# Order of the vector and scalar engines' work on the first two pairs of the up projection

## What is computed

```python
h = rms_norm_2(x, norm_mlp[l])
x = x + jnp.square(jax.nn.relu(h @ w_up[l])) @ w_down[l]
```

## Time and profile before

| | |
|---|---|
| median of 3 executions | 2404.96 us (2403.06 to 2407.01) |
| the profiled execution | 2402.84 us |
| its span, first to last instruction | 2401.0 us |
| TensorE busy in the span | 2358.2 us (98%) |
| VectorE, ScalarE, GpSimd busy | 1635.9, 1065.7, 963.7 us |
| granted TensorE clock, mean | 0.998 |

### The profile page before, as it was taken

How to read it: one execution, slowest core, us unless ns; L and a number is a source line. 1 busy time by engine, 2 the same in 40 slices (tenths; PEclk the granted TensorE clock), 3 DMA queues, 4 the chain that set the end, 5 groups by cost and what they waited for, 6 DMA issues and landing times.

```text
span 2401.0 us, 31551 instructions
## 1 busy us (share of the span) xinstructions
PE 2358.2 (98%) x11548; PEld 1871.2 (78%) x11548; DVE 1635.9 (68%) x2026; ACT 1065.7 (44%) x1628; POOL 963.7 (40%) x535
## 2 busy tenths in 40 slices
PE   9999999999999999999999999999999999999997
PEld 6888658887777777777788777788877888888886
DVE  6999975467647466475866555555688777637994
ACT  5555562335544545456442333223354444443344
POOL 2899833332222222222233111222346555465564
PEclk9999999999999999999999999999999999999999
DMA  3111333221111111111032111221125666886764
GB/s 138 44 44 52 105 140 123 79 95 45 45 41 41 41 41 45 41 41 41 27 113 66 49 40 35 82 71 45 53 114 155 153 153 160 227 294 238 276 240 146
DMA packets 112116, 238.76 MB, mean 99 GB/s; under 512 B 42360, under 2 KB 45304, under 8 KB 111992
## 3 DMA queue, kind: packets, MB, share of 16 engines
q1 hardware_dynamic: 73040, 216.28, 28.0%
q10 hardware_dynamic: 38952, 20.76, 3.9%
HBM read 184.44 MB, written 46.27 MB: 96 GB/s over the span
## 4 chain that ended last, share of the span: by engine, by line
PE 80%; DVE 8%; issue 4%; ACT 3%; POOL 3%; DMA 1%; ACTq 0%; SPq 0%; DVEq 0%; POOLq 0%
PE ps_A L897 23%; PE ps_B L897 22%; PE ps_A L1435 8%; PE ps_B L1435 8%; PE ps_C L1435 4%; PE ps_D L1435 2%; POOL ta L800 1%; PE ps_C L917 1%; PE ps_B L1179 1%; PE ps_D L1005 1%; PE ps_C L1071 1%; POOL accp L800 1%; PE ps_D L1071 1%; PE ps_D L1164 1%; PE ps_D L1152 1%
## 5 line engine op out<-in xcount | busy, mean ns | idle before, releaser
L774 POOL CAST w_hi<-w_raw 128x1024 fp32r<-128x1024 f32 x98 | 107.7, 1099 | 1059.1 <-PE ps_A L897 483.9
L767 POOL TENSOR_TENSOR w_lo<-w_raw,w_hi 128x1024 fp32r<-128x1024 f32 x124 | 307.4, 2479 | 49.6 <-ACT w_hi L1580 41.8
L862 POOL TENSOR_TENSOR down_w_lo<-d_raw,down_w_hi 128x512 fp32r<-128x512 f32 x112 | 179.3, 1620 | 136.1 <-ACT down_w_hi L2271 136.1
L897 PE MATMUL ps_A<-HA_hi,w_hi 128*128 128x512 f32 x640 | 201.2, 395 | 4.0 <-POOL w_lo L767 2.2
L897 PE MATMUL ps_B<-HA_hi,w_hi 128*128 128x512 f32 x640 | 202.2, 397 | 2.9 <-POOL w_lo L767 1.5
L897 PE MATMUL ps_B<-HA_lo,w_hi 128*128 128x512 f32 x640 | 197.5, 390 | 0.0
L897 PE MATMUL ps_A<-HA_lo,w_hi 128*128 128x512 f32 x640 | 197.4, 390 | 0.0
L897 PE MATMUL ps_B<-HA_hi,w_lo 128*128 128x512 f32 x640 | 197.3, 389 | 0.0
L897 PE MATMUL ps_A<-HA_hi,w_lo 128*128 128x512 f32 x640 | 197.3, 389 | 0.0
L897 PEld LDWEIGHTS ps_A<-HA_hi,w_hi 128*128 128x128 f32 x640 | 117.1, 188 | 29.7 <-issue 3.9
L897 PEld LDWEIGHTS ps_B<-HA_lo,w_hi 128*128 128x128 f32 x640 | 120.1, 188 | 25.6
(11 more groups left out here) (510 smaller groups left out, 5956.9 us busy)
## 6 DMA issues: line engine op xcount, KB each, us to landing
w_raw<-w_dram SPq DMA_DIRECT2D x124, 512.0 KB, 3.3
d_raw<-w_dram SPq DMA_DIRECT2D x64, 512.0 KB, 4.6
t_raw<-u_dram SPq DMA_DIRECT2D x56, 512.0 KB, 6.0
a_raw<-w_dram SPq DMA_DIRECT2D x32, 512.0 KB, 7.6
u_dram<-b SPq DMA_DIRECT2D x56, 256.0 KB, 5.2
u_dram<-t SPq DMA_DIRECT2D x48, 256.0 KB, 6.8
X<-x_dram SPq DMA_DIRECT2D x16, 512.0 KB, 7.1
d_raw<-w_dram SPq DMA_DIRECT2D x32, 256.0 KB, 3.0
```

Source lines behind the costliest of these rows:

```text
L767: pool.tensor_tensor(w_lo[q][:, :, :], w_raw[q][:, :, :], w_hi[q][:, :, :].bitcast(F32), ALU.subtract).then_inc(S[f"w_ready{q}"], 1)
L774: pool.tensor_copy(w_hi[q][:, :, :], w_raw[q][:, :, :]).then_inc(S["w_rounded"], 1)
L862: pool.tensor_tensor(lo[:, :, :], d_raw[i % 3][:, down_parts(x), :], hi[:, :, :].bitcast(F32), ALU.subtract).then_inc(S["down_split"], 1)
L897: op = pe.matmul(AB[b][:, cols], wt[:, w0 + k, :], act[:, k, cols], start=(first and k == ks[0] and step == 0), stop=(last and k == ks[-1] ...
```

## The change

On VectorE, `form_s2_s3(1)` moves from behind the last two activation splits to just behind `form_s4(0)`, ahead of the four `scaled_lo(3, j)`; it is given a wait for the sum (0,3), since it overwrites `s2`, which `form_s4(0)` reads. `form_t(0)` moves from the pass i = 1 of the loop (behind `c12_c21(0)`) into the pass i = 2, behind `c22(1)` and `r22(1)`. On ScalarE, `round_up(9)`, `(10)` and `(11)` each come one step sooner: 9 ahead of the first rounding of T2, 10 ahead of the second, and 11 ahead of the squares of pair 0 and `keep_p5(1)`. SyncE's, GpSimd's and TensorE's lists stay as they are.

```diff
             round_up(8)
+            round_up(9)
             round_two(4, T2[:, 0:2, :], 0)
-            round_up(9)
+            round_up(10)
             round_two(4, T2[:, 2:4, :], 1)
-            round_up(10)
             act.wait_ge(S["up_out"], OUT_AT[("c11", 0)] + 1)
             keep_p1(1)
+            round_up(11)
             squared(b11, 0, "r11")
             squared(b22, 0, "r22")
             keep_p5(1)
-            round_up(11)
...
             form_s4(0)
+            dve.wait_ge(S["up_sum"], SUM_AT[(0, 3)] + 1)
+            form_s2_s3(1)
             for j in range(KH):
                 scaled_lo(3, j, x_half(2 * j + 1, 1), 2 * j + 1)
...
-            form_s2_s3(1)
             next_cd()
...
                     r22(i - 1)
+                if i == 2:
+                    form_t(0)
                 form_s4(i)
                 c12_c21(i - 1)
-                form_t(i - 1)
+                if i > 1:
+                    form_t(i - 1)
                 if i < UP_PAIRS - 1:
                     form_s1(i + 1)
                     form_s2_s3(i + 1)
```

## The result

| | before | after |
|---|---|---|
| median (executions) | 2405.69 us (16) | 2410.24 us (16) |
| lowest to highest | 2402.43 to 2409.63 | 2408.92 to 2413.29 |
| span of the profiled execution | 2401.0 us | 2409.8 us |
| mean granted TensorE clock in it | 0.998 | 0.996 |

The ratio is 1.0020, 95% interval 1.0014 to 1.0027: slower by about 4.6 us, 0.19%. The two profiled spans are further apart, 8.8 us.

What follows compares the result with a forecast made beforehand. TensorE, with work in 98% of the span, was taken as the bound, hanging at product 18 on `form_t(0)`; 5.8 us of delay and 2.1 of clock made 7.9 us, median 2412.9 us, range 2406.5 to 2416.

Steps and rivals of the forecast that it cites:

- The chain: Up projection: product 18 hangs without slack on the end of `form_t(0)`, via stores, load of pair 3 and ScalarE; 15.06 us.
- Part 1: Head of the up projection: second pair's sums and roundings sooner; worth -0.25 us, bounds +0.4 and -1.6.
- Part 2: `form_t(0)` moved behind the read out of pair 1: ends at 1812.5, 5.8 us later; no stop before product 14.
- The count by turns: VectorE at `form_t(0)`: its four instructions take 2.7 us plus three turns with GpSimd's splits, after two turns ahead of it.
- The DMA term: Landing of the pair 3 loads behind the stores: change taken as 0, bounds -1 and +1 us.
- The clock: Behind the 8 us stop before product 18, TensorE falls to 1.2 GHz; return costs 2.1 us, bounds 0 and 3.
- The sum: Whole execution: 5.8 us of delay plus 2.1 of clock make 7.9 us, profiled 2410.7 us, median 2412.9.
- the milder rivals: Smaller losses: clock up or fewer turns, 2410 us, chance 0.25; VectorE ahead of GpSimd, 2405.8 us, chance 0.14.
- the forecast's own: Whole kernel: late `form_t(0)` and fallen clock as forecast, 2412.9 us, range 2410.5 to 2416, chance 0.55.
- rival 2: Same delay at product 18, but the clock stays up or VectorE meets fewer turns: 4 to 6 us, 2410 us, chance 0.25.
- The fourth: Faster: `form_t(0)` ends at 1807.5, load lands sooner, product 18 comes 0.3 to 0.8 us sooner; 2404.4 us, chance 0.06.
- the head's gain: Ahead of product 18, at the stops before products 10, 11 and 14: 1.7 us won, then swallowed by the stop.

Runs made afterwards that it cites:

- e1_after_loads_first: Changed kernel with SyncE issuing the two loads of pair 3 ahead of the five stores of pair 0; median 2405.09 us, ratio 1.0001 to the kernel before.
- e3_part2: Kernel before with only `form_t(0)` moved behind `c22(1)` and `r22(1)`; median 2410.51 us, ratio 1.0027 to the kernel before.
- e2_part1: Changed kernel with `form_t(0)` put back where it was; median 2404.51 us, ratio 0.9997 to the kernel before.
- e6_splits_behind: Changed kernel with ScalarE rounding operands 16 and 17 only behind the square of 12 of pair 1; median 2409.12 us, ratio 1.0016 to the kernel before.
- the filler: Changed kernel with 24 more matmuls, results unread, on TensorE right behind product 17; median 2408.68 us, ratio 1.0014 to the kernel before.
- e4_before_loads_first: Kernel before with SyncE issuing the loads of pair 3 ahead of the five stores of pair 0; median 2404.73 us, ratio 0.9997.

## Why the prediction was right, and where it was off

**The chain.** It was right in each link: product 18 hung on the end of `form_t(0)` through SyncE's queue and the load of pair 3, and `e1_after_loads_first` shows it by taking the load out, `e3_part2` by moving that step alone.

**Part 1** was put at -0.25 us, a small loss, and measured 0.0: in `e2_part1` product 11 starts at 36.72 instead of 36.79, and the median is level. The turning of a wait for GpSimd into one for VectorE came as told, product 9 stopping for both halves of its operand.

**Part 2, the end of `form_t(0)`.** Predicted 1812.5, 5.8 us late; measured 1813.43, less the 0.60 us by which the execution began later, 1812.83: 6.1 us late. The count by turns held, and `e6_splits_behind` shows that it is the turns. The Trainium skill, page "SBUF — State Buffer", section "Who interferes with whom", says that a VectorE instruction with two SBUF inputs and a GpSimd one that reads SBUF exclude each other for a whole instruction. The trace agrees: `form_t(0)` takes 5.8 us with three splits beside it and 3.7 with one. The split that took 4.09 us takes 4.08 us in the changed kernel too, and no run explains it.

**The DMA term** was mis-sized: I took 0 against the 9.7 us of the earlier trace rows, and the second load landed in 8.2 us, 1.5 us less (8.1 and 8.3 in `e3_part2` and `e6_splits_behind`, 9.7 in `e2_part1`, where `form_t(0)` stays). Why it lands sooner there is not shown. So the start of product 18 moved by 4.68 us, not 5.8.

**The clock** was put at 2.1 us, from the weight loads of the earlier trace rows. From product 18 to the start of the down projection the changed kernel took 2.77 us more than the kernel before, and with the filler nothing more. In `e3_part2` it took 2.07 us more, so the term varies. That the clock falls in all 16 executions is likely, since their mean clocks are 0.995 to 0.997, but the mean alone doesn't prove it: a quarter of the executions of the kernel before show 0.996 or 0.997 too. The Trainium skill, "TensorE: Matmul & The Clock Gate", section "HAM oscillation — how this bites in real kernels", says that waits between bursts of matmuls bring the clock down; here one wait of 6.55 us did.

**The sum** for one execution was 7.9 us; from the first product to the end it measured 8.20: 4.68 to product 18, 2.77 by the clock up to the beginning of the down projection, and 0.75 behind that, mostly in the stops there, which vary by as much from one execution of the kernel before to the next. That 7.9 and 8.20 are so close is in part luck: the DMA term was 1.5 us too high, the clock 0.7 too low, and the 0.75 was not in the sum. The step that failed is the last one: I carried the difference of single executions over to the medians, and the medians are only 4.6 us apart. The profiled execution of the kernel before lies 2.85 us under the median of its 16, that of the changed kernel 1.35 us above. The prediction took 2.12 us for the first, as for a fixed offset, and nothing for the second. A difference of two profiled executions carries the distance of both from their medians, here 4.2 us together. My range held the result only because it reached down to the milder rivals: 2410.24 us lies just under the forecast's own 2410.5 to 2416 and on the 2410 us of rival 2, though neither of that rival's conditions (a clock that stays up, fewer turns) came. The mechanism is the forecast's, the number is the rival's. Whether the change is slower by over 0.2%, to which I gave 0.77, is not decided: the interval runs from 0.14 to 0.27%.

**The rivals.** The fourth claimed that nothing short of loads that pass the stores would let the head's gain through. With loads that pass the stores it still didn't get through: the wait of `keep_p5(2)` for the stores themselves stood next, and the prediction had not listed it. A stall that goes uncovers the next one in the same in-order queue; I had followed only the first.

## What to carry to other kernels

Before a step is moved back, follow what is issued after it in every in-order queue, the DMA queue first: here four vector instructions carried five stores, two loads and, behind them, the copy that TensorE waits for. Where such a queue puts loads that are needed soon behind stores that nobody needs, turn the order round before anything else; then read which wait comes next in the same engine's list, since two edits were needed here and one gave nothing. And a long stop of TensorE must be priced with the slow matmuls behind it: here 6.55 us of standing cost a further 2.77.

## What the runs showed of the hardware

- The two loads of pair 3, 512 KB each, landed in 3.6 to 4.4 us with no stores close by in the queue (`e1_after_loads_first`), in 4.0 and 5.7 us with five stores of 256 KB issued 1.15 us behind them (`e4_before_loads_first`), and in 7.5 to 9.7 us right behind those five stores (the kernels before and changed). The order doesn't only shift their start, it doubles their time on the way.
- A stop of TensorE of 6.55 us brought the clock from 2.4 to 1.2 GHz in the middle of a kernel that was otherwise busy, and matmuls started 0.427 us apart until about 6 us after the restart; behind the stop of 6.16 us in `e3_part2` it was 4 us. Stops of 2.27 and 3.37 us left it up in the profiled executions of `e1_after_loads_first` and `e6_splits_behind`.
